# Projection filler in steps of two rows of weights instead of one, in a hybrid attention layer

## The reference, cut to what matters

```python
h = rmsnorm(x, norm_g)                      # x: (1, 1024, 1024) float32
proj = jnp.einsum('bsd,dp->bsp', h, w_in)   # q, k, v, gate of three groups, f_logit
o_sb = stick_breaking_attention(q_sb, k_sb, v_sb)          # weights by a reverse cumulative sum of logs
o_ch = chunked_relpos_attention(rmsnorm(q_ch), rmsnorm(k_ch), v_ch, rel_bias)   # softmax over a band
o_fx = forgetting_attention(rmsnorm(q_fx), rmsnorm(k_fx), v_fx, log_f)          # causal softmax with decay
mixed = concat([o_sb * silu(g_sb), o_ch * silu(g_ch), o_fx * silu(g_fx)])
return x + jnp.einsum('bsm,md->bsd', mixed, w_out)
```

## Time and profile before

| | us |
|---|---|
| median of 3 runs (1044.59 to 1045.76) | 1045.06 |
| the profiled execution | 1045.31 |
| its span, first to last instruction | 1043.5 |
| PE busy, 5816 matmuls | 1015.7 |
| token products of the projection, line 1216, x2304 | 478.5 |
| gate products, line 1220, x576 | 157.1 |
| transposes of `turn`, line 1290, x816 | 125.4 |
| `values`, line 1308, x576 | 140.2 |
| DVE busy | 682.6 |
| ACT busy | 632.2 |

### The profile page before, as it was taken

The page is one execution under the profiler, slowest core; times in us unless marked ns, Lnnn a source line. Parts: engine busy times, 40 slices in busy tenths (PEclk is TensorE's granted clock), DMA queues, the critical chain, the costliest instruction groups (busy, mean ns, idle before and its releaser), DMA issues.

```text
span 1043.5 us, 16263 instructions
## 1 busy us (share of the span) xinstructions
PE 1015.7 (97%) x5816; PEld 911.2 (87%) x5816; DVE 682.6 (65%) x1304; ACT 632.2 (61%) x1232; POOL 102.1 (10%) x90
## 2 busy tenths in 40 slices
PE   6999999999999999999999999999999998999998
PEld 6988989899899998998998998998998986787787
DVE  5656675765866667667557548879789787877100
ACT  6658775776767767758667667556567555553000
POOL 1210201101211011011012001011010010000000
PEclk9999999999999999999999999999999999999999
DMA  8254151431522513314314204204214228732941
GB/s 251 83 139 117 36 152 42 113 104 33 136 80 66 137 42 107 96 52 130 84 40 127 77 21 115 68 22 127 56 30 121 61 64 253 207 102 83 302 131 38
DMA packets 112944, 105.50 MB, mean 101 GB/s; under 512 B 10048, under 2 KB 83784, under 8 KB 112864
## 3 DMA queue, kind: packets, MB, share of 16 engines
q1 hardware_dynamic: 110784, 104.43, 36.3%
q10 hardware_dynamic: 2080, 0.04, 0.1%
HBM read 62.44 MB, written 19.98 MB: 79 GB/s over the span
## 4 chain that ended last, share of the span: by engine, by line
PE 82%; DVE 8%; DMA 4%; ACT 3%; issue 2%; SPq 0%; POOL 0%; ACTq 0%; DVEq 0%; POOLq 0%
PE psP L1216 37%; PE psO L1308 9%; PE psP L1220 8%; PE psT L1290 8%; PE psS L1268 4%; PE psS L1269 4%; PE psP L1356 2%; PE psS L1356 2%; PE psP L1326 2%; PE psT L1238 2%; PE psO L1356 2%; DVE big L1001 1%; DVE rb L1120 1%; PE psS L1273 1%; DMA stack<-mixed_scratch 1%
## 5 line engine op out<-in xcount | busy, mean ns | idle before, releaser
L1216 PE MATMUL psP<-big 128*128 128x384 f32 (+1 forms) x2304 | 478.5, 345 | 1.8 <-DVE big L1001 1.4
L1216 PEld LDWEIGHTS psP<-big 128*128 128x128 f32 x2304 | 394.9, 189 | 8.5 <-DVE big L1001 1.7
L1131 DVE TENSOR_TENSOR pt<-psT,pt 128x512 fp32r<-128x512 f32 (+1 forms) x224 | 143.4, 642 | 140.5 <-ACT pt L943 139.5
L943 ACT ACTIVATE pt<-psT 128x512 fp32r<-128x512 f32 (+1 forms) x224 | 125.1, 559 | 117.2 <-PE psT L1290 116.9
L1220 PE MATMUL psP<-big 128*128 128x512 f32 x576 | 157.1, 405 | 0.0
L1308 PE MATMUL psO<-pt,vst 128*128 128x512 f32 (+3 forms) x576 | 140.2, 343 | 6.3 <-DVE pt L1131 5.7
L1290 PE MATMUL psT<-identr,z 128*128 128x128 f32 x816 | 125.4, 272 | 0.0
L1220 PEld LDWEIGHTS psP<-big 128*128 128x128 f32 x576 | 102.4, 189 | 18.1
L1290 PEld LDWEIGHTS psT<-identr,z 128*128 128x128 f32 x816 | 101.6, 140 | 15.3
L1308 PEld LDWEIGHTS psO<-pt,vst 128*128 128x128 f32 x576 | 99.2, 189 | 17.8 <-issue 8.6
L1104 DVE CUSTOM_DVE_ANT_0 z<-psS,rb 128x640 f32<-128x640 f32 (+7 forms) x128 | 89.4, 699 | 35.7 <-PE psS L1269 17.3
(11 more groups left out here) (113 smaller groups left out, 1097.4 us busy)
## 6 DMA issues: line engine op xcount, KB each, us to landing
stack<-stack SPq DMA_DIRECT2D x192, 128.0 KB, 2.3
wraw<-in_w_in_dram SPq DMA_DIRECT2D x90, 192.0 KB, 2.6
wraw<-in_w_in_dram SPq DMA_DIRECT2D x24, 256.0 KB, 3.3
mixed_scratch<-mst SPq DMA_DIRECT2D x24, 256.0 KB, 2.4
mixed_scratch<-gate SPq DMA_DIRECT2D x24, 256.0 KB, 2.6
wraw<-in_w_out_dram SPq DMA_DIRECT2D x24, 256.0 KB, 3.2
rb<-decay_scratch SPq DMA_DIRECT2D x8, 512.0 KB, 4.1
big<-mixed_scratch SPq DMA_DIRECT2D x8, 512.0 KB, 6.1
```

Source lines behind the costliest of these rows:

```text
L943: nc.scalar.activation(pt[:, ci % PTR, 0, 0:w], psT[:, m % NT, 0:w], ACT.Copy).then_inc(s_hi, 1)
L1131: nc.vector.tensor_tensor(pt[:, ci % PTR, 1, 0:w], psT[:, m % NT, 0:w], pt[:, ci % PTR, 0, 0:w].bitcast(F32), ALU.subtract).then_inc(s_eva ...
L1216: ins = nc.tensor.matmul(dst[:, 0:TOKW - first], hT[a][:, k, i * P:(i + 1) * P], wpair[b][:, k, first:TOKW], start=(k == 0 and q == 0), st ...
```

## The change

The filler's pieces are two rows of weights (six matmuls) where they were one (three), with twice the estimated cost. The products, their order within the projection and the waits are the same. A line is added, so each line of the kernel behind it has a number one higher.

```diff
-        for k in range(KT):
-            steps = [("project", jj, gi, k, k + 1)]
-            if k == KT - 1:
+
+        for k in range(0, KT, 2):
+            steps = [("project", jj, gi, k, k + 2)]
+            if k == KT - 2:
                 steps.append(("raw", jj, i) if kind == "t" else ("gate", jj, i))
-            out.append((steps, 3 * (NS["narrow"] if kind == "t" else NS["step"]), kind if k == KT - 1 else ""))
+            out.append((steps, 6 * (NS["narrow"] if kind == "t" else NS["step"]), kind if k == KT - 2 else ""))
```

## The result

The changed kernel takes 1049.85 us in the median of 7 runs (1047.42 to 1052.34), the kernel before 1045.35 us in the median of 7 beside it (1043.54 to 1048.0): the ratio is 1.0039, with a 95% interval of 1.0022 to 1.0057. It is 4.1 us slower (0.0039 x 1045), between 2.3 and 6.0. The profiled execution of the changed kernel is the quickest of the seven, 1047.42 us with a span of 1045.6, so it shows less of the loss than the median does: 2.1 us of span.

The account below looks back on a forecast made before the run. PE, busy 97% of the span, was taken as the bound, so the price lies in its waits; the terms summed to +3.7 us, forecast 1048.8 us (0.36% slower), own range 1047.5 to 1050.2, whole range 1044.8 to 1051.0.

Parts of the forecast that it names:

- Pairs 1 to 3: At `heads`: late squares delay DVE's scaling, so PE waits; 0.85 us each, 2.55 us in all.
- Pair 4: At the first turn's `values`: DVE 0.82 us later, partly covered because `values` start 0.28 us later; 0.57 us lost.
- Pairs 5 to 7: At `values`: low part 1.15 us later, 0.71 us covered by added products; 0.44 us lost each, 1.32 us in all.
- Lost cover elsewhere: Exchanged order takes cover from `values` in pairs 4 to 10; between -0.5 and +0.8 us, taken as nothing.
- Pair 8: No squares, but a 1.15 us exponential exchanged; less ACT's idle 0.22 and 0.71 of products, 0.22 us lost.
- Pairs 9 and 10: No exponential there; added products fill a wait of 0.65 us in each, -1.30 us in all.
- Pair 0: Transposes of `heads` 0.71 us later, so SP issues the next pair's last weight load later; 0.5 us lost.
- Pair 11: `values` wait about 0.8 us, only shortening the 3.69 us load wait; copies start earlier, -0.2 us.
- The clock: Rival: pair 11's wait shortens to some 2.7 us and the clock may stay up, 1047.2 us; chance 0.28.
- the first two cases: The forecast itself, 1048.8 us, chance 0.40, and the rival that the clock holds, 1047.2 us, chance 0.28.
- absorbed queues: Rival: ACT or DVE makes up the delay before `norm` and first low part; only cover counts, 1041.9 us; chance 0.13.
- The swallowed loss: Rival: pair 11's awaited load does not move with PE's work, its wait hides the loss; 1045.1 us, chance 0.12.

Follow-up runs that it names:

- `fine_gate`: Changed kernel with all eight exponentials ahead of the last copy and gate groups in single pieces; run once, 1045.42 us, without a comparison of times.
- `first_two`: Kernel before, with only the first piece of the second gate half two rows long in pairs 5 to 10; 1041.41 us against 1045.70, ratio 0.9957.
- `only_9_10`: Kernel before, with double pieces only in the fillers of pairs 9 and 10; 1044.22 us, ratio 0.9971.
- `warm_less`: Kernel before, with 5 extra products ahead of the long wait at `first` in pair 11; 1045.42 us, ratio 0.9998.
- `exps_ahead`: Changed kernel with the eight exponentials of pairs 1 to 8 back ahead of the last token group's copy; 1044.83 us, ratio 0.9989.

## Why the prediction was right, point by point

The forecast was 1048.8 us, slower, for the late exponential; measured were 1049.85 us, slower, and the exponential is shown as the cause by putting it back and by moving it alone. The steps, in the order of the prediction:

- **Pairs 1 to 3, 0.85 us each: 0.76 us each.** The mechanism and the place are as put: squares late, DVE without a gap, a new wait of `heads` behind the scaling. The delay was sized by the duration of the exponential (0.82 us); the step was mis-sized because rows of ACT overlap: the exponential starts 0.39 us after the copy, where the squares needed 0.52, and the squares 0.81 us after the exponential, which leaves a delay of 0.68 us. By the table of starts it is 2.09 us in all (-0.39 to 1.70) where the sum had 2.55.
- **Pair 4, 0.57 us: 0.53 us** at the first `values` of unit 15.
- **Pairs 5 to 7, 0.44 us each: 0.28, 0.28 and 0.29 us** more at the first `values`, for the same reason: 1.15 us were put in for the exponential, the squares of pair 7 are 1.00 us later, and three products cover 0.71 of that. But from the first `values` of unit 15 to score row 116 the table of starts has 2.97 us (2.24 to 5.21; 0.52 by unit 17 and 2.45 in pairs 5 to 7), not 1.32.
- **Lost cover elsewhere, taken at nothing: this is the step that failed.** I had gone no further than the first `values` of each unit. The fourth `values` of units 17, 19, 23 and 27 wait 0.64, 0.41, 0.68 and 0.40 us, and score row 100 waits 0.42 us for keys. They cost 2.1 us (the 2.97 above less 0.85 at the first `values`); the prediction's bounds for this term, -0.5 to +0.8 us, did not hold it. `fine_gate` and `first_two` together show that the three products taken from ahead of the fourth turn are the cause at units 19, 23 and 27. At unit 17 it is six products of 384 columns that no longer stand between the third turn and the fourth `values`, which fits, but no run gave them back there.
- **Pair 8, 0.22 us: 0.11 us** (0.36 at the first `values` of unit 31, before 0.25), and 0.06 in the table.
- **Pairs 9 and 10, -1.30 us: -1.27 us** (5.27 to 4.00), and `only_9_10` has the gain alone.
- **Pair 0, 0.5 us: 0.14 us.** PE waits 1.70 us for the last row of weights, from start to start, before 1.56. The later issue of the load, which the prediction put in, does not show: `heads` starts 0.25 us later (62.17, now 62.42), but SP issues the load 0.43 us earlier (66.20, now 65.77).
- **Pair 11, -0.2 us:** PE came to the long wait 4.93 us late, waited 2.08 us in place of 3.94, and left it 3.07 us late. PE came so late because the loss of 4.00 us at score row 164 was joined by the new wait at the first `values` of unit 43 (0.86 us), which the prediction had at 0.8. The long wait gave back 1.86 us in all, where the prediction had 0.8 us of wait and 0.2 us of earlier load. Behind it, the next group waits 2.00 us for DVE's sum, before 0.73.
- **The clock.** Both of the first two cases came to pass. The profiled execution kept the full clock through the wait of 2.08 us, at 1047.42 us; the rival had 1047.2. The other six runs had a mean clock of 0.997 or 0.998 and took 1048.93 to 1052.34 us. The nearness of 1047.42 to the rival's number is partly luck: in that execution the held clock shortened the way from the second group of `first` to the fifth by 0.57 us, not by 1.64, since DVE's sum became what PE waited for.

Of the rivals, absorbed queues fall with the earlier trace rows read beside the same rows of after: DVE has no gap that gives the delay back. The swallowed loss falls too, as the load of pair 11 came 3.07 us later, though the wait for it took back 1.86 of the 4.93 us. The sum was better than its terms: up to score row 164 it had 3.86 us and the traces show 4.00, but that is luck: the 1.6 us missing in pairs 5 to 7 and at unit 17 were made up by terms taken too large (0.5 in pairs 1 to 3, 0.2 in pair 8) and by 0.9 us at unit 0, where the sum has 0.5 us of loss and the profiled execution of the changed kernel was 0.4 us ahead.

## What to carry to other kernels

In a list that several engines walk in step, ask for every moved product whose cover it was, up to the last use in the unit and not only the first; and see what else the new boundaries exchange on the other engines. Here eight exponentials that slid by one place behind a copy cost 5 us, more than all the moved products were worth. Moving only the products around the wait that they fill, in six pairs, with every other step left where it stood, gave 4.5 us (2.7 to 6.3). And cost a moved instruction by what it puts between the starts of its neighbours, 0.68 us here, not by the length of its row, 0.82 us.

## What the runs showed of the hardware

- Idle times of PE of 3.40 to 4.12 us in pair 11 were followed by the lower clock (0.50, which is 1.2 of 2.4 GHz) in all six profiles that have one. Of eight idle times between 1.8 and 2.3 us in pair 11 it fell after four (2.10, 2.11, 2.19 and 2.28 us) and held after four (1.83, 1.84, 2.01 and 2.18 us). It held after three more of about this length at score row 20 (1.79, 1.88 and 1.95 us). At an idle time of some 2 us the same kernel comes out either way, as six to six in `warm_less`. The earlier trace rows have a wait of 1.40 us, after which it held. But in `exps_ahead` it fell in pair 0 with idle times of 1.02 and 0.39 us ahead of the fall, which twelve other profiles have without one. So the forecast's comparison of 2.7 us with 3.69 and with nothing was no guide: in these runs the length of one idle time alone does not tell whether the clock falls.
- Full clock in a run of one kernel goes with some 1.5 us less: of the 70 runs of the kernel before, the six at 1.000 have a median of 1044.6 us, the 57 at 0.997 or 0.998 one of 1046.1. This is no proof that the clock saves it all, as a run with shorter waits keeps its clock more often.
- ACT's idle time before its copies of token groups rose from 65.3 us in 52 waits to 101.3 us in 78, and nothing followed from it except where the queue behind a copy was needed by DVE: idle time of an engine that does not bound tells nothing until one names the instruction behind it.
